# Two placements in on-chip memory: x's high and low parts, and the block weights, in the perceptrons of a three-layer kernel

## The reference, cut to what matters

```python
def squared_relu_mlp(h, w1, w2):
    a = jax.nn.relu(h @ w1)
    return (a * a) @ w2
...
        h = rmsnorm_2(x, norm_gains[layer, 1])
        x = x + squared_relu_mlp(h, mlp_w1[layer], mlp_w2[layer])
```

## The kernel before

| tile | start before | mod 128 | start after | mod 128 | mod 256 after |
|---|---|---|---|---|---|
| weight_hi0, weight_lo0 (and the other slots) | 33280, 49664 | 0 | the same | 0 | 0 |
| a_hi, in the perceptrons | 82432 | 0 | 82496 | 64 | 64 |
| a_lo, in the perceptrons | 98816 | 0 | 99008 | 64 | 192 |
| a_hi, in the other stages | 82432 | 0 | 82432 | 0 | 0 |
| a_lo, in the other stages | 98816 | 0 | 98944 | 0 | 128 |
| scratch (high token sums) | 115264 | 64 | 115392 | 64 | 192 |
| block_low (low token sums) | 199232 | 64 | 199232 | 64 | 64 |
| block_weight, _hi, _lo | 177728, 183872, 190016 | 64 | 177664, 183808, 189952 | 0 | 0 |
| hidden_hi, hidden_lo | 140800, 157184 | 0 | the same | 0 | 0 |

## Time and profile before

### The profile page before, as it was taken

How to read it: one execution, slowest core, us unless ns; L and a number is a source line. 1 busy time by engine, 2 the same in 40 slices (tenths; PEclk the granted TensorE clock), 3 DMA queues, 4 the chain that set the end, 5 groups by cost and what they waited for, 6 DMA issues and landing times.

```text
span 1904.6 us, 28284 instructions
## 1 busy us (share of the span) xinstructions
PE 1861.1 (98%) x10454; PEld 1571.7 (83%) x10454; DVE 1050.7 (55%) x1863; ACT 853.6 (45%) x1562; POOL 1087.2 (57%) x1321
## 2 busy tenths in 40 slices
PE   8999999999999999999999999999999999999998
PEld 6878777888888888878888999878887888999887
DVE  6647764521223377775755555485755576555552
ACT  4555455632323366665443444344433354444341
POOL 5427333455557433426788888644433278888882
PEclk9999999999999999999999999999999999999999
DMA  6214212133333221212333232332222133332331
GB/s 190 59 34 125 61 50 66 51 83 100 100 101 110 86 58 57 67 34 78 90 105 105 89 111 89 108 93 76 67 67 56 45 100 100 100 100 89 100 111 55
DMA packets 269162, 160.42 MB, mean 84 GB/s; under 512 B 6137, under 2 KB 267489, under 8 KB 268898
## 3 DMA queue, kind: packets, MB, share of 16 engines
q1 hardware_dynamic: 269026, 158.61, 29.0%
HBM read 156.50 MB, written 2.10 MB: 83 GB/s over the span
## 4 chain that ended last, share of the span: by engine, by line
PE 85%; POOL 5%; DVE 4%; ACT 3%; issue 2%; DMA 0%; ACTq 0%; DVEq 0%; SPq 0%
PE bank L259 19%; PE bank L2004 9%; PE bank L622 7%; PE bank L623 7%; PE bank L624 7%; POOL weight_lo L241 3%; PE bank L2649 3%; PE bank L2651 3%; PE bank L2650 3%; PE bank L1602 2%; PE bank L424 2%; PE bank L1604 2%; PE bank L1603 2%; PE bank L426 2%; PE bank L425 2%
## 5 line engine op out<-in xcount | busy, mean ns | idle before, releaser
L241 POOL TENSOR_TENSOR weight_lo<-weight_stage,weight_hi 128x256 fp32r<-128x256 f32 x1160 | 963.7, 864 | 736.3 <-ACT weight_hi L229 736.2
L229 ACT ACTIVATE weight_hi<-weight_stage 128x1024 fp32r<-128x1024 f32 (+2 forms) x303 | 309.1, 1022 | 254.6 <-PE bank L259 180.5
L259 PE MATMUL bank<-hidden_hi,weight_lo 128*128 128x512 f32 x512 | 200.4, 391 | 4.9 <-POOL weight_lo L241 4.9
L622 PE MATMUL bank<-a_hi,weight_lo 128*128 128x512 f32 (+1 forms) x464 | 197.7, 426 | 2.0 <-POOL weight_lo L241 1.2
L259 PE MATMUL bank<-hidden_lo,weight_hi 128*128 128x512 f32 x512 | 199.4, 389 | 0.0
L259 PE MATMUL bank<-hidden_hi,weight_hi 128*128 128x512 f32 x512 | 199.2, 389 | 0.0
L623 PE MATMUL bank<-a_lo_rounded,weight_hi 128*128 128x512 f32 (+1 forms) x464 | 182.3, 393 | 0.0
L624 PE MATMUL bank<-a_hi,weight_hi 128*128 128x512 f32 (+1 forms) x464 | 182.1, 392 | 0.0
L1980 POOL TENSOR_TENSOR block_weight_lo<-block_weight,block_weight_hi 128x256 fp32r<-128x256 f32 x156 | 124.7, 831 | 52.7 <-ACT block_weight_hi L2139 52.7
L2354 DVE TENSOR_TENSOR x_t<-x_t,bank 128x512 f32<-128x512 f32 x128 | 82.1, 678 | 90.3 <-PE bank L259 90.3
L259 PEld LDWEIGHTS bank<-hidden_hi,weight_lo 128*128 128x128 f32 x512 | 96.2, 188 | 25.9 <-issue 6.9
(11 more groups left out here) (393 smaller groups left out, 4374.1 us busy)
## 6 DMA issues: line engine op xcount, KB each, us to landing
weight_stage<-in_mlp_w SPq DMA_DIRECT2D x128, 512.0 KB, 3.8
weight_stage<-in_w_in SPq DMA_DIRECT2D x57, 512.0 KB, 3.7
weight_stage<-in_hg_w_in SPq DMA_DIRECT2D x32, 512.0 KB, 3.9
weight_stage<-in_sb_w_qkv SPq DMA_DIRECT2D x24, 512.0 KB, 3.6
weight_stage<-in_w_mkv SPq DMA_DIRECT2D x8, 512.0 KB, 3.9
weight_stage<-in_w_out SPq DMA_DIRECT2D x8, 512.0 KB, 3.8
weight_stage<-in_sb_w_o SPq DMA_DIRECT2D x8, 512.0 KB, 3.8
weight_stage<-in_hg_w_o SPq DMA_DIRECT2D x8, 512.0 KB, 3.9
```

What stands on the lines that cost most here:

```text
L229: act.activation(self.hi[slot][:, 0:size], self.stage[slot][:, 0:size], ACT.Copy).then_inc(self.hi_done, 1)
L241: last = pool.tensor_tensor(self.lo[slot][:, part], self.stage[slot][:, part], self.hi[slot][:, part].bitcast(F32), ALU.subtract)
L259: last = pe.matmul(out, l, r, start=n == 0, stop=n == 3 * len(pairs) - 1)
L622: pe.matmul(to, wlo, ahi(k), start=k == 0, stop=False)
```

## The change

The two tiles for x's parts become longer (by 32 and by 16 floats), and each has two views of the same shape: one at the tile's start, one 64 bytes further. The perceptrons' two norms write the view further on, and the perceptrons read it; the three other norms and stages keep the view at the start. The filler of 64 bytes that stood ahead of the block weights is moved behind them, so that the sums of weights lie at multiples of 128 while `block_low` stays where it was. `a_lo`, `scratch` and the small tiles behind it (`const`, `cos`, `sin`, `kpe_sq` and others) move by 128 bytes, and a filler is cut by as much, so that everything from `hidden_hi` on keeps its place. On each of the five engines the instructions, their order, their shapes and their waits are the same before and after; the addresses alone differ.

```diff
-FIRST_GAP, HALF_LINE, SECOND_GAP = 96, 16, 64
+FIRST_GAP, HALF_LINE, SECOND_GAP = 96, 16, 32
...
-    def __init__(self, S, gain, bank, added, before, writes=1, spreads=2):
+    def __init__(self, S, gain, bank, added, before, writes=1, spreads=2, ahi=None, alo=None):
         self.S, self.gain, self.bank, self.squares = S, gain, bank, S.scratch
+        self.ahi, self.alo = (S.ahi, S.alo) if ahi is None else (ahi, alo)
...
-        act.activation(S.ahi[:, t, :], S.x[:, t, :], ACT.Copy, scale=self.gain_column(t)).then_inc(self.hi_done, 1)
+        act.activation(self.ahi[:, t, :], S.x[:, t, :], ACT.Copy, scale=self.gain_column(t)).then_inc(self.hi_done, 1)
...
-        sb("block_half_line", [P, HALF_LINE])
         wsum = sb("block_weight_", [P, 3, 4 * P])
         whi = sb("block_weight_hi_", [P, 3, 4 * P], F32R)
         wlo = sb("block_weight_lo_", [P, 3, 4 * P], F32R)
         kept = sb("block_kept_", [P, 3, HALF])
+        sb("block_half_line", [P, HALF_LINE])
...
-                return [(S.ahi[:, a + k, half], S.alo[:, a + k, half]) for k in range(4)]
+                return [(norm.ahi[:, a + k, half], norm.alo[:, a + k, half]) for k in range(4)]
...
-        S.ahi = S.sb("a_hi", [P, ND, T], F32R)
-
+
+        def placed(space, start):
+            return space[:, start:start + ND * T].rearrange("p (c t) -> p c t", c=ND)
+        a_hi = S.sb("a_hi", [P, ND * T + 2 * HALF_LINE], F32R)
...
-        S.alo_f, S.alo = pair(S.sb, "a_lo", ND)
-        S.sb("half_line", [P, HALF_LINE], F32)
+        with nc.sbuf_tensor("a_lo_rounded", [P, ND * T + HALF_LINE], F32R) as a_lo:
+            pass
+        S.alo_f = placed(S.sb("a_lo", [P, ND * T + HALF_LINE], F32), 0)
+        S.ahi, S.alo = placed(a_hi, 0), placed(a_lo, 0)
+        S.ahi_beyond, S.alo_beyond = placed(a_hi, HALF_LINE), placed(a_lo, HALF_LINE)
...
-        mlp_norm = FoldedNorm(S, g2 + 8, S.ps[7], S.x_added, ND)
+        mlp_norm = FoldedNorm(S, g2 + 8, S.ps[7], S.x_added, ND, 1, 2, *beyond)
...
-        mlp2_norm = FoldedNorm(S, g2 + 24, S.ps[7], S.x_added, 2 * ND)
+        mlp2_norm = FoldedNorm(S, g2 + 24, S.ps[7], S.x_added, 2 * ND, 1, 2, *beyond)
```

More of the change, by code:

```diff
@@ L357, in dve_tile @@
         dve.wait_ge(self.hi_done, tiles + t + 1)
-        dve.scalar_tensor_tensor(out=S.alo[:, t, :], in0=S.x[:, t, :], scalar=self.gain_column(t),
-                                 in1=S.ahi[:, t, :].bitcast(F32), op0=ALU.mult,
+        dve.scalar_tensor_tensor(out=self.alo[:, t, :], in0=S.x[:, t, :], scalar=self.gain_column(t),
+                                 in1=self.ahi[:, t, :].bitcast(F32), op0=ALU.mult,
                                  op1=ALU.subtract).then_inc(self.lo_done, 1)
@@ L1991, in up_whole @@
                         pe.wait_ge(evicted, whole_done(r - 4))
-                    products(pe, S.ps[r % 4][:, :], ((W.tile(b + r, k), (S.ahi[:, k, :], S.alo[:, k, :]))
+                    products(pe, S.ps[r % 4][:, :], ((W.tile(b + r, k), (norm.ahi[:, k, :], norm.alo[:, k, :]))
                                                  for k in range(ND)), (lambda k: norm.ready(pe, k)) if r == 0 else None
@@ L2151, in high_x @@
                     act.wait_ge(W.used, u0 + WHOLE)
-                    act.activation(S.ahi[:, 0:4, right], t4, ACT.Copy).then_inc(kept_done, 1)
+                    act.activation(norm.ahi[:, 0:4, right], t4, ACT.Copy).then_inc(kept_done, 1)
                 else:
@@ L2238, in lower_x @@
                 if n == 3:
-                    dve.tensor_tensor(S.alo[:, 0:4, right], t4, S.ahi[:, 0:4, right].bitcast(F32),
+                    dve.tensor_tensor(norm.alo[:, 0:4, right], t4, norm.ahi[:, 0:4, right].bitcast(F32),
                                       ALU.subtract).then_inc(evicted, 1)
@@ L3021, in build @@
         sb_norm = FoldedNorm(S, g2, S.ps[6], S.x_added, 0, 1, 0)
-        mlp_norm = FoldedNorm(S, g2 + 8, S.ps[7], S.x_added, ND)
+        beyond = S.ahi_beyond, S.alo_beyond
+        mlp_norm = FoldedNorm(S, g2 + 8, S.ps[7], S.x_added, ND, 1, 2, *beyond)
         hg_norm = FoldedNorm(S, g2 + 16, S.ps[7], S.shared("mlp_added")[0], 56, 2)
-        mlp2_norm = FoldedNorm(S, g2 + 24, S.ps[7], S.x_added, 2 * ND)
+        mlp2_norm = FoldedNorm(S, g2 + 24, S.ps[7], S.x_added, 2 * ND, 1, 2, *beyond)
         first, first_out = first_block(S, w, consts, opening, sb_norm)
```

## The result

The changed kernel takes 1911.06 us in the median of ten runs (1907.1 to 1912.29), the kernel before 1906.08 us beside it on the same chip (ten runs, 1903.99 to 1908.33). The ratio is 1.0023, with a 95% interval of 1.0015 to 1.0031: 5.0 us slower, where the forecast was 8.0 us faster. Its profiled execution took 1911.52 us for a span of 1909.7 us, 5.1 us longer than the span before.

The account below looks back on a forecast made before the run. TensorE's matmul pace was taken to bound the kernel, with a chain of other engines setting twelve waits. Gains of 5.4 + 1.9 + 0.3 + 0.5 = 8.0 us gave 1898.2 us from 1906.17, range 1893.5 to 1903.2.

Parts of the forecast that it names:

- The price of a block: Perceptron blocks of 256 columns: all run at m5's 113.4 ns, 11.6 us over 26 pairs, not all arriving.
- The rival of a longer period: Perceptron blocks: period 256, streams at 192 priced at 117.9 ns; 4.9 us faster, 1901.3 us; chance 0.21.
- The 128 bytes by which `a_lo`, `scratch` and the small tiles move elsewhere I price at nothing.: Tiles displaced by the edit: no cost, between bounds of 1904.2 and 1892.2 us.
- takes back elsewhere: Rival: 912 `a_lo` matmuls outside the perceptrons, each 6.6 ns dearer, lose 6.0 us; chance 0.10 shared with one slowed piece.
- The long matmuls: 288 matmuls of 512 columns in `up_whole`: 144 count, gain between 0 and 0.95 us, taken as 0.5.
- L2649, L1602 and L622 should keep their means: Sign in the changed kernel's profile: these lines of 512-column matmuls keep their mean lengths.
- The wait: TensorE before twelve later `down` runs: wait grows from 0.57 to 0.88 us, losing 3.8 us of the gain.
- a longer chain of 1.0 us each: Rival: slowed GpSimd pieces lengthen the twelve chains before the `down`; with three, 14.8 us, 1913.0 us; chance 0.05.
- Writers and GpSimd: ScalarE and VectorE writers of moved tiles and GpSimd's pieces on the sums of weights: no cost.
- The rule of independent ports: Skill's rule for TensorE: separate read ports, so positions can't matter and the sum is zero; does-nothing rival, 1906.2 us, chance 0.04.

Follow-up runs that it names:

- e5: No kernel: matmuls of 256 columns alone, in paired runs of 24 with operands at 0 or 64; the same 64 by 0 took 117.9 or 113.3 ns.
- e12: No kernel: matmuls of 256 columns alone, one operand stepped 64 bytes from distance 0; up gave 117.7 to 117.8 ns, down 113.3 to 113.4.
- e3: Kernel before with only the sums of weights moved to 0; 1906.33 us, ratio 0.9998.
- e1: No kernel: matmuls alone, runs of 24 at 512 and 256 columns, with moving tile and weights at many placements; 227.1 to 233.3 ns at 512 columns.
- e2: Kernel before with only the displacement: `a_lo` at 128 and `scratch` at 192 modulo 256, small tiles going along; 1912.48 us, ratio 1.0032.
- e10: Kernel before with `a_lo` at 128 modulo 256, `scratch` and small tiles keeping their places modulo 256; 1912.28 us, ratio 1.0037.
- e4: Changed kernel without the displacement: `a_lo` at 0 modulo 256 outside the perceptrons, 64 in them, `scratch` at 64; 1906.22 us, ratio 1.0002.
- e6: Changed kernel with `a_lo` at 0 modulo 256 outside the perceptrons, 64 inside, `scratch` at 64, and sums of weights back at 64; 1905.23 us, ratio 0.9992.
- e8: The places of e4 plus the edit of e7 (early high part of the last sum of weights); 1895.35 us, ratio 0.9942 against the kernel before.
- e9: The places of e6 plus the edit of e7 (early high part of the last sum of weights); 1892.99 us, ratio 0.9936 against the kernel before.
- e11: Kernel before with `a_lo` left, `scratch` moved to 192 and the small tiles by 128 bytes; 1907.37 us, ratio 1.0007.
- e7: Kernel before, addresses untouched, with ScalarE making the last sum of weights' high part ahead of the squares; 1897.86 us, ratio 0.9954.

## Why the prediction was wrong

*The price of a block: the step that failed.* "I price them by m5's 113.4 ns." The number was right for m5, and the reason wrong. At distance 64 or 192, 256 columns have two paces, 117.8 and 113.3 ns, and the way in chooses (e5, e12). The term that this fed, 11.6 us for the blocks, measured 2.2 us. Before the change m5 was entered from m7, at 64 by 64, by weights going down to 0. The change put the sums of weights at 0, which took that step away: e3 shows it alone. Six of seven blocks so gained 0 to 3 ns instead of 4.4 to 6.6, and m5 lost 4.4.

*The rival of a longer period.* It had the right period, 256, and `a_lo` in its list. But I read it out of m5 and m3 (113.3 and 118.3 ns in the earlier trace rows), as 64 being cheap and 192 not, and so it came to 4.9 us faster. Those two differ by direction: m5's weights step down, m3's step up. At 256 columns 64 and 192 cost the same (e1), and m3 at 192 could have been fast. The argument was a comparison of two blocks with different neighbours.

*"The 128 bytes by which `a_lo`, `scratch` and the small tiles move elsewhere I price at nothing."* The second step that failed. e2 and e10 measured 6.5 and 7.0 us for it. The rival "takes back elsewhere" had the 912 matmuls and 6.0 us from them, against 5.6 us in the trace. The place was right; that the size fits is luck in part, as its 6.6 ns were the difference of two blocks of 256 columns. My reason against it, that tiles at different residues modulo 2048 run alike, was worth nothing: all of them that follow one another in longer runs start 226 to 229 ns apart in the trace before, and e1's pace at distance 128 is 232.4, so none of them had tried that place.

*The long matmuls.* 0.5 us of gain were taken for 64 by 0. e1 has 228.9 ns there against 227.1 at 0, so a loss; in the change, where x's low part is at 192, `up_whole` went to 230.2, and 1.0 us was lost in it. "L2649, L1602 and L622 should keep their means" holds for the lengths in L622 (427 ns) and L2649 (423, then 424), not in L1602 (417, then 422); and it was the wrong sign to name, since the loss sits in the lines with `a_lo` and in the distances.

*The wait.* Right. Gains between m3a and the `down` vanish into it (e4, e6), and without it they arrive (e8, e9). I had put it from 0.57 to 0.88 us; it went to 0.70, as the gains were small, and not all of the rise is theirs: from m4a to the `down` it takes 7.77 us in the changed kernel, 7.68 before, so the chain itself grew by 0.09 us, about 1.0 us over twelve. The chain after shows which step grew, against 1.89 us in the earlier trace rows:

```profile
980.61 1.99 POOL block_weight_lo L1981 x2
```

These two GpSimd pieces take 1.89 us in each of the twelve chains before and 1.99 in each after; the other steps keep their lengths within 0.01 us, but for the four pieces behind them in two of the chains, 0.1 us longer. The way from m4a to the `down` follows them in the other runs: 1.89 us and 7.68 in e3, 1.89 and 7.67 in e11, 1.94 and 7.73 in e6, 2.00 and 7.78 in e4 and e10; in e2, with 1.99 and 7.86, the four pieces behind them grew by 0.1 us as well. The place of the sums of weights isn't what does it, as e3 moved them and kept 1.89. Beside these pieces VectorE makes `hidden_lo` from `sin`, and that goes the other way: 0.93 to 0.94 us in the mean in the kernel before, e3 and e11, 0.72 to 0.74 in the changed kernel, e2, e4, e6 and e10. Why the two trade, and why the placement decides it, isn't shown. The chances gave "slower" 0.05, for a longer chain of 1.0 us each; it grew by a tenth of that, and the loss came from elsewhere.

*Writers and GpSimd.* Priced at nothing. ScalarE is busy 853.4 us against 853.6, VectorE 1039.6 against 1050.7 and GpSimd 1089.7 against 1087.2, most of it beside TensorE; the tenth of a microsecond in the chain, just told, is where GpSimd did cost something.

*The rule of independent ports.* The Trainium skill, page "TensorE: Matmul & The Clock Gate", section "Step-by-step: what each phase is for", gives the streamed operand and the weights a read port each. The runs don't agree that they never meet: distance alone makes 227.1 or 233.3 ns in e1. I had weighed this rightly and still drew the wrong law from two blocks.

## What to carry to other kernels

A pace read from one block is that block's with its neighbours: before pricing others by it, run the matmuls by themselves at every placement and in the order in which they will follow one another. When tiles are moved for one stage, count who else streams from them, by the distance in bytes from the weights to the moving operand, modulo 256. And where a chain of other engines ends last, shorten the chain first (e7, one line moved, 8.0 us); a faster TensorE pays only behind that.

## What the runs showed of the hardware

- The spacing of float32r matmuls, each with its own weights, depends on the distance from weights to moving operand modulo 256 bytes: at 512 columns 227.1, 228.9, 232.4 and 233.3 ns for 0, 64, 128 and 192 (e1).
- Where every third matmul streams from a tile at distance 128 and the others from one at 0, all take 233.3 ns on average, not the 228.9 of the mean (e1, and `up_whole` in e2 and e10).
- At 256 columns distance 0 has 119.7 to 120 ns and is the dearest, the reverse of 512 columns; at 64 and 192 there are two lasting paces, 117.8 and 113.3. From distance 0 a step of one operand 64 bytes up enters the slow one, 64 bytes down the fast one (e5, e12, 8 of 8 tests there); from distance 128 a step up entered the fast one in one test of seven in e1 and in e5's only one, both at the same places, so the full rule isn't known. The fast pace is 4% under the slow one, 5% under that of distance 0.
- The slow pace lasted over 192 matmuls. In e12 six matmuls at distance 0 ended it, in e5 twelve did not; what decides was not found.
